# Cached keys of a decode attention step: 32x32 block loads turned by VectorE in place of TensorE transposes

## The reference, cut to what matters

```python
h = rmsnorm(x, g_mix_pre)
proj = h @ w_in                       # q, k, v, xr, gb, gates
k_past = cache_k[l][page_table].reshape(Bs, past_len, N_HEADS, HEAD_DIM)
v_past = cache_v[l][page_table].reshape(Bs, past_len, N_HEADS, HEAD_DIM)
k_all = concatenate([k_past, k]); v_all = concatenate([v_past, v])
logits = einsum('bhqd,bhqjkd->bhqjk', q, kg) * (HEAD_DIM ** -0.5) + bias   # T5 relative bias, masked
p = softmax(logits); o_attn = einsum('bhqjk,bhqjkd->bhqd', p, vg)
o_rnn = rglru(conv(xr)) * gelu(gb)
merged = sigmoid(gate_a) * (o_attn @ w_pa) + sigmoid(gate_r) * (o_rnn @ w_pr)
x = x + rmsnorm(merged @ w_out, g_mix_post)
x = x + rmsnorm((silu(g_) * u_) @ w_down, g_ffn_post)      # from f = rmsnorm(x) @ w_gate_up
```

## Time and profile before

| | |
|---|---|
| runs, median (range) | 795.58 us (795.12 to 795.71) |
| the profiled execution, its own time | 790.97 us |
| its span, first to last instruction | 789.2 us |
| busy: TensorE (PE) | 774.7 us, 98% of the span |
| busy: VectorE (DVE), ScalarE (ACT), GpSimd (POOL) | 473.6, 359.6, 64.4 us |
| TensorE's mean granted clock | 0.997 of full speed |
| DMA traffic | 89.21 MB, mean 113 GB/s |

### The profile page before, as it was taken

One profiled execution on the slowest core, in us unless ns is written; L12 is line 12 of the kernel. 1 busy time (PEld: TensorE's weight loads), 2 busy tenths in 40 slices (PEclk: granted clock), 3 DMA queues, 4 the chain that ended last, 5 costly groups with the idle time before them and its releaser, 6 DMA issues.

```text
span 789.2 us, 16457 instructions
## 1 busy us (share of the span) xinstructions
PE 774.7 (98%) x6100; PEld 735.3 (93%) x6100; DVE 473.6 (60%) x741; ACT 359.6 (46%) x624; POOL 64.4 (8%) x149
## 2 busy tenths in 40 slices
PE   8999999999999999999999999999999999999996
PEld 7988988999899899997799999999999999999995
DVE  5665656746637634774567987778777784222223
ACT  6336435634634632334456555545555563223232
POOL 4501102102011010004000000000000010000000
PEclk9999999999999999999999999999999999999998
DMA  7765235345323224615551333322333143222312
GB/s 213 198 183 157 81 108 149 97 114 132 105 80 82 79 86 129 192 54 180 167 167 47 108 107 106 98 86 84 104 106 106 53 155 106 75 82 84 92 54 114
DMA packets 155201, 89.21 MB, mean 113 GB/s; under 512 B 17093, under 2 KB 148633, under 8 KB 155162
## 3 DMA queue, kind: packets, MB, share of 16 engines
q1 hardware_dynamic: 152350, 81.63, 35.6%
q0 software_dynamic: 2576, 6.45, 2.4%
q10 hardware_dynamic: 236, 0.61, 0.3%
HBM read 81.85 MB, written 6.81 MB: 112 GB/s over the span
## 4 chain that ended last, share of the span: by engine, by line
PE 94%; SPq 3%; issue 1%; DVE 1%; ACT 1%; DMA 0%; DVEq 0%; ACTq 0%
PE ps L865 33%; PE ps L1210 27%; PE ps L1275 17%; PE ps L1109 6%; PE ps L1179 3%; PE ps L964 1%; PE ps L978 1%; PE ps L995 1%; PE ps L937 1%; SPq L563 1%; SPq L569 1%; SPq L553 1%; PE ps L1043 1%; PE ps L1117 1%; PE ps L1008 1%
## 5 line engine op out<-in xcount | busy, mean ns | idle before, releaser
L1821 DVE TENSOR_TENSOR w_lo<-w_raw,w_hi 128x1024 fp32r<-128x1024 f32 (+1 forms) x68 | 80.9, 1192 | 131.0 <-ACT w_hi L1352 130.7
L865 PE MATMUL ps<-xin_hi,w_hi 128*128 128x272 f32 x576 | 126.1, 298 | 0.9 <-DVE xin_lo L1844 0.9
L1352 ACT ACTIVATE w_hi<-w_raw 128x1024 fp32r<-128x1024 f32 (+1 forms) x68 | 69.9, 1030 | 118.6 <-PE ps L1275 82.6
L865 PE MATMUL ps<-xin_hi,w_lo 128*128 128x272 f32 x576 | 120.4, 288 | 0.0
L865 PE MATMUL ps<-xin_lo,w_hi 128*128 128x272 f32 x576 | 120.2, 288 | 0.0
L865 PEld LDWEIGHTS ps<-xin_hi,w_hi 128*128 128x128 f32 x576 | 90.1, 189 | 9.2 <-issue 7.6
L865 PEld LDWEIGHTS ps<-xin_lo,w_hi 128*128 128x128 f32 x576 | 91.0, 188 | 0.0
L865 PEld LDWEIGHTS ps<-xin_hi,w_lo 128*128 128x128 f32 x576 | 90.6, 189 | 0.0
L1275 PE MATMUL ps<-hid_hi,w_hi 128*128 128x272 f32 x352 | 76.0, 291 | 0.4 <-DVE hid_lo L2215 0.4
L1275 PE MATMUL ps<-hid_lo,w_hi 128*128 128x272 f32 x352 | 74.9, 287 | 0.0
L1275 PE MATMUL ps<-hid_hi,w_lo 128*128 128x272 f32 x352 | 74.9, 288 | 0.0
(11 more groups left out here) (338 smaller groups left out, 1756.8 us busy)
## 6 DMA issues: line engine op xcount, KB each, us to landing
w_raw<-in_w_in_dram SPq DMA_DIRECT2D x72, 256.0 KB, 3.2
g_raw<-in_w_gate_up_dram SPq DMA_DIRECT2D x40, 256.0 KB, 3.9
w_raw<-in_w_down_dram SPq DMA_DIRECT2D x40, 256.0 KB, 2.9
u_raw<-in_w_gate_up_dram SPq DMA_DIRECT2D x20, 256.0 KB, 3.1
e_raw<-in_w_gate_up_dram SPq DMA_DIRECT2D x20, 256.0 KB, 4.3
kc<-in_cache_k_dram SPq DMA_DIRECT2D x64, 64.0 KB, 2.1
vc<-in_cache_v_dram SPq DMA_DIRECT2D x64, 64.0 KB, 2.0
wo_raw<-in_w_out_dram SPq DMA_DIRECT2D x12, 256.0 KB, 3.8
```

The costliest lines, as they stand in the source:

```text
L865: mm = e.matmul(ps[:, bank + h, 0:HT], wt[:, kw, :], xt[:, kx, h * HT:h * HT + HT], start=first and wt is wh and xt is xh, stop=last and ( ...
L1352: e.activation((to or w_hi[s])[:, 0:k, :], w_raw[s][:, 0:k, :], ACT.Copy).then_inc(hi_done, count)
L1821: e.tensor_tensor(wl[:, 0:k, :], w_raw[s][:, 0:k, :], wh[:, 0:k, :].bitcast(F32), ALU.subtract).then_inc(lo_done, count)
```

## The change

The keys of pairs 1 to 3 are no longer turned by TensorE. `load_keys` loads a page so that the partition is 32 x (feature block) + (token // 4) and the row holds 4 tokens x 32 features: the source pattern is 4 blocks x 128 tokens x 32 features, in runs of 128 bytes. `keys_turn(f)` on VectorE then turns 32x32 blocks, four pages in one instruction of 128x512, straight from `kc` to `kcT`. In `kcT` token 4i+a of a page then stands at column 32a+i. The bias is copied into that order (4 GpSimd copies for one), the value pages are loaded in that order (4 x 32 rows of 512 bytes), and pair 0, whose keys are still loaded by rows and turned by TensorE, writes the order when it leaves PSUM. A semaphore `kc_turned` takes over from the counts of T_BANK. The key pages of the next pair are issued a few behind each weight tile: in pair 0 four each behind tiles 4 to 7, in pairs 1 and 2 behind tiles 2 to 7 (2, 3, 3, 3, 3, 2), and the wait ahead of them is for this pair's four turns. In pair 0 the groups and `scores_s` stand a little earlier between the matmuls.

```diff
@@ constants @@
-TP_IT = 5 + len(PT_USES)
+TP_IT = 1 + len(PT_USES)
+BLK = 32
+KC_PAGES = (), (), range(0, 2), range(2, 5), range(5, 8), range(8, 11), range(11, 14), range(14, 16)
+KC_PAGES_0 = (), (), (), (), range(0, 4), range(4, 8), range(8, 12), range(12, 16)
@@ helpers @@
+        def cache_cols(f):
+            return kcT[:, 2 * f:2 * f + 2, :].rearrange("p b (n a i) -> p (b n) i a", n=NPG, i=BLK)
+        def cache_turned():
+            return ps[:, T_BANK, :].rearrange("p (n i a) -> p n i a", n=4, i=BLK)
@@ SyncE @@
-            def load_pages(cache, dst, done, it, part):
+            def page_of(cache, it, j):
+                return cache[0].rearrange("n t h d -> n t (h d)")[bass.ds(page[j], 1), :, bass.ds(it * P, P)]
+            def load_keys(it, pages):
+                for j in pages:
+                    e.dma_start(kc[:, j, :], page_of(cache_k, it, j).rearrange("o t (b c) -> b (o t) c", c=BLK)
+                                ).then_inc(kc_in, 16)
+            def load_keys_0():
+                for j in range(DEC_B * NPG):
+                    e.dma_start(kc[:, j, :], page_of(cache_k, 0, j).rearrange("o t c -> t (o c)")).then_inc(kc_in, 16)
+            def load_values(it, part):
                 for j in range(8 * part, 8 * part + 8):
-                    src = cache[0].rearrange("n t h d -> n t (h d)")[bass.ds(page[j], 1), :, bass.ds(it * P, P)]
-                    e.dma_start(dst[:, j, :], src.rearrange("o t c -> t (o c)")).then_inc(done, 16)
+                    e.dma_start(vc[:, j, :], page_of(cache_v, it, j).rearrange("o (i a) c -> a (o i) c", i=BLK)
+                                ).then_inc(vc_in, 16)
...
-                    if j in (5, 6) and not last:
-                        e.wait_ge(s_ready, it * 5 + 1)
-                        load_pages(cache_k, kc, kc_in, it + 1, j - 5)
+                    pages = (KC_PAGES_0 if first else KC_PAGES)[j]
+                    if pages and not last:
+                        e.wait_ge(kc_turned, it * 4 + 4)
+                        load_keys(it + 1, pages)
@@ GpSimd @@
-            e.tensor_copy(bias_s[:, :, 0:PAST], bias_rev[:, :, DEC_T:DEC_T + PAST][:, :, ::-1]).then_inc(consts, 1)
+            for f in range(PAIRS):
+                src = bias_rev[:, f, DEC_T:DEC_T + PAST][:, ::-1].rearrange("p (n i a) -> p n a i", n=NPG, i=BLK)
+                e.tensor_copy(bias_s[:, f, 0:PAST].rearrange("p (n a i) -> p n a i", n=NPG, i=BLK), src).then_inc(consts, 1)
@@ TensorE @@
                 def cache_T(f):
                     if f == 0:
-                        e.wait_ge(kc_in, it * 256 + 256)
-                    tp_wait(f)
+                        e.wait_ge(kc_in, 256)
+                    else:
+                        e.wait_ge(kc_turned, f)
...
-                    cache_T(1); begin(2); part(2, 0, 2); cache_T(2); part(2, 2, 4); cache_T(3); part(2, 4, 8); scores_s()
+                    cache_T(1); begin(2); part(2, 0, 1); cache_T(2); part(2, 1, 3); cache_T(3); part(2, 3, 6)
+                    scores_s(); part(2, 6, 8)
                 else:
-                    begin(0); part(0, 0, 4); cache_T(0); part(0, 4, 8)
-                    begin(1); cache_T(1); part(1, 0, 4); cache_T(2); part(1, 4, 8)
-                    begin(2); cache_T(3); part(2, 0, 5); scores_s(); part(2, 5, 8)
+                    begin(0); part(0, 0, 8)
+                    begin(1); part(1, 0, 8)
+                    begin(2); part(2, 0, 5); scores_s(); part(2, 5, 8)
@@ VectorE @@
+                def keys_turn(f):
+                    if f == 0:
+                        e.wait_ge(kc_in, it * 256 + 256)
+                        e.wait_ge(pv_done, it)
+                    e.transpose(kcT[:, 2 * f:2 * f + 2, :].rearrange("p b k -> p (b k)"),
+                                kc[:, 4 * f:4 * f + 4, :].rearrange("p n c -> p (n c)")).then_inc(kc_turned, 1)
...
                 else:
-                    next_lo(0); cache_copy(1)
-                    next_lo(1); cache_copy(3)
+                    next_lo(0)
+                    keys_turn(0); keys_turn(1)
+                    next_lo(1)
+                    keys_turn(2); keys_turn(3)
                     next_lo(2)
                     k_copy()
```

More of the change, by code:

```diff
@@ L92 @@
 C_ZERO = 8
-C_BIAS = C_ZERO + 1 + DEC_B + 2 * PAIRS
+C_BIAS = C_ZERO + PAIRS + DEC_B + 2 * PAIRS
+BLK = 32
+KC_PAGES = (), (), range(0, 2), range(2, 5), range(5, 8), range(8, 11), range(11, 14), range(14, 16)
+KC_PAGES_0 = (), (), (), (), range(0, 4), range(4, 8), range(8, 12), range(12, 16)
 SERIES = 9
@@ L355, in program @@
         kc_in = sem("kc_in")
+        kc_turned = sem("kc_turned")
         vc_in = sem("vc_in")
@@ L594, in iteration @@
                     if j in (2, 4) and first:
-                        load_pages(cache_v, vc, vc_in, 0, (j - 2) // 2)
-                    if j in (5, 6) and not last:
-                        e.wait_ge(s_ready, it * 5 + 1)
-                        load_pages(cache_k, kc, kc_in, it + 1, j - 5)
+                        load_values(0, (j - 2) // 2)
+                    pages = (KC_PAGES_0 if first else KC_PAGES)[j]
+                    if pages and not last:
+                        e.wait_ge(kc_turned, it * 4 + 4)
+                        load_keys(it + 1, pages)
                 e.wait_ge(mi_free, it * 6 + 3)
@@ L613, in iteration @@
                     e.wait_ge(mi_ready, it * 6 + 3)
-                    load_pages(cache_v, vc, vc_in, it + 1, 0)
-                    load_pages(cache_v, vc, vc_in, it + 1, 1)
+                    load_values(it + 1, 0)
+                    load_values(it + 1, 1)
             load(2, 0, wi[:, :, 2 * 512:2 * 512 + P])
-            for part in range(2):
-                load_pages(cache_k, kc, kc_in, 0, part)
+            load_keys_0()
             load(3, 1, wi[:, :, 3 * 512:3 * 512 + P])
@@ L758, in _ @@
                 own = bias_s[:, f, PAST:KS].rearrange("p (j g t) -> p j g t", j=NJ, g=NG)
-                e.wait_ge(consts, C_ZERO + 1 + DEC_B + 2 * f)
+                e.wait_ge(consts, C_ZERO + PAIRS + DEC_B + 2 * f)
                 e.affine_select(out=own, in_=own, compare_op=ALU.is_ge, fill=NEG,
                                 base=0, pattern=[[-8, NJ], [-GR, NG], [0, DEC_T]], channel_multiplier=1).then_inc(consts, 1)
-                e.wait_ge(consts, C_ZERO + 2 + DEC_B + 2 * f)
+                e.wait_ge(consts, C_ZERO + PAIRS + 1 + DEC_B + 2 * f)
                 e.affine_select(out=own, in_=own, compare_op=ALU.is_ge, fill=NEG,
@@ L933, in cache_T @@
                     if f == 0:
-                        e.wait_ge(kc_in, it * 256 + 256)
-                    tp_wait(f)
+                        e.wait_ge(kc_in, 256)
+                    else:
+                        e.wait_ge(kc_turned, f)
                     for n in range(4):
                         mm = e.transpose(ps[:, T_BANK, n * P:n * P + P], kc[:, 4 * f + n, :], ident[:, :])
-                    mm.then_inc(tp_ready, 1)
+                    mm.then_inc(small_T, 1)
                 def scores_s():
@@ L944, in scores_s @@
                     e.wait_ge(mi_free, it * 6 + 1)
-                    tp_wait(4)
+                    e.wait_ge(kc_turned, it * 4 + 4)
                     e.wait_ge(logits_done, it * 9 + 1)
@@ L973, in probs_T @@
                     e.wait_ge(scaled, it * 8 + (unit(qt, 1 if both else hs) + 1))
-                    tp_wait(5 + n)
+                    tp_wait(1 + n)
                     for i, h in enumerate(range(2) if both else (hs,)):
@@ L983, in probs_T_s @@
                     e.wait_ge(probs_done, it + 1)
-                    tp_wait(4)
+                    tp_wait(0)
                     for n in range(NPG):
@@ L1402, in cache_copy @@
                 def cache_copy(f):
-                    e.wait_ge(tp_ready, it * TP_IT + (f + 1))
-                    e.activation(kcT[:, 2 * f:2 * f + 2, :], ps[:, T_BANK, :].rearrange("p (b k) -> p b k", b=2),
-                                 ACT.Copy).then_inc(tp_free, 1)
+                    e.wait_ge(small_T, f + 4)
+                    e.activation(cache_cols(f), cache_turned(), ACT.Copy).then_inc(kc_turned, 1)
                 def exp_s():
@@ L1418, in probs_copy @@
                     qt, hs = PT_USES[n]
-                    e.wait_ge(tp_ready, it * TP_IT + (5 + n + 1))
+                    e.wait_ge(tp_ready, it * TP_IT + (n + 2))
                     if hs == 2:
@@ L1441, in heads @@
                     e.activation(sp[2][:, :], sp[1][:, :], ACT.Exp, scale=-1.0).then_inc(sp_act, 1)
-                cache_copy(0)
+                    cache_copy(0)
                 next_hi(1)
@@ L1446, in heads @@
                 e.activation(halves(qT[:, :]), two(0), ACT.Copy, scale=DH ** -0.5).then_inc(tile_free[0], 1)
-                cache_copy(2)
+                if first:
+                    cache_copy(2)
                 next_hi(2)
@@ L1453, in heads @@
                 e.activation(halves(vT[:, :]), two(0), ACT.Copy).then_inc(tile_free[0], 1)
```

(13 more changed lines are left out.)

1 line of the change is left out of this document (removed).

## The result

The changed kernel takes 814.2 us (median of 4, 812.5 to 814.6) against 795.35 for the kernel before: 1.0244 times as long, interval 1.021 to 1.0279. The forecast was 813.

What follows compares the result with a forecast made beforehand. TensorE, busy 98% of the span, was taken as the bound. Terms -6.0 + 13.5 + 8.4 + 2 gave +18 us: 809 on the profiled execution, 813 on the median of 795.6; range 792 to 842.

Steps and rivals of the forecast that it cites:

- Transposes removed: On TensorE, twelve groups of transposes go at 0.45 us each: 5.4 us gained.
- pair 0's new order: In pair 0, the 0.86 us wait is covered, `cache_T(2)` waits some 0.3 us: net 0.6 us gained.
- VectorE and GpSimd: Four turns of 0.71 us a pair and four bias copies cost nothing; GpSimd's bounds 0 and 1 us.
- Four engines: On the page loads, 4 of 16 DMA engines carry each page; chance 0.58 at about 12 to 18 ns, 800 to 842.
- Pair 0: Full DMA queue makes TensorE wait at `probs_T(2)` and at pair 1's tiles 0 and 1: 13.5 us.
- Tile 1's 2.0: At pair 1's tile 1, ready at 105.1 where TensorE wants it at 103.1: 2.0 us more wait.
- The price of a small row: A load of a 128-byte row takes one DMA engine 12 ns, with bounds 12 and 25 ns.
- Pairs 1 and 2: Late tile 3 load makes `scores_s` wait 3.7 us, the next tile 0 costs 0.5: 8.4 us for both pairs.
- Clock: After a TensorE wait of 9 us some matmuls run at 1.2 GHz: 2 us, bounds 0 and 5.
- The first rival: Sixteen engines carry a page, nothing queues, `scores_s` waits 2.2 us a pair: -1.6 us, 794 (791 to 797); chance 0.32.

Runs made afterwards that it cites:

- experiment 5: Changed kernel with all pages by whole rows on sixteen engines and no key page ahead of tile 3's load: 785.9 us, ratio 0.9936.
- experiment 1: Changed kernel with all key and value pages moved by whole 512-byte rows on sixteen engines: 794.4 us, ratio 1.0029.
- experiment 2: Changed kernel with only the value pages by whole rows on sixteen engines, keys still on four: 799.15 us, ratio 1.0087.
- experiment 3: Changed kernel with only the key pages of pairs 1 to 3 by whole rows on sixteen engines, values still on four: 794.8 us, ratio 1.0035.
- experiment 4: As all pages on sixteen engines, but key pages of pairs 1 to 3 in 128-byte rows, tokens outermost: 794.8 us, ratio 1.0032.
- the last version: Changed kernel, values and bias in cache order, scores written at stride 4, no key page ahead of tile 3's load, next tile 0's load before value pages: 788.8 us.
- experiment 6: Changed kernel with one edit, no key page ahead of tile 3's load: 806.9 us, ratio 1.0181.
- experiment 7: Changed kernel with the next pair's tile 0 load issued ahead of its 16 value pages: 806.1 us, ratio 1.0185.
- experiment 8: Changed kernel with TensorE's waits filled by extra transposes of the identity: 815.9 us, ratio 1.0301.
- the version of 793.0 us: Changed kernel, values and bias in cache order, turned keys read at stride 32, no key page ahead of tile 3's load: 793.0 us, ratio 1.0006.
- the one with quarters: Values and bias in cache order, each key page of pairs 1 to 3 fetched by four transfers, no key page ahead of tile 3's load: 864.0 us, ratio 1.0905.

## Why the prediction was right, and where it was off

By its steps, against the profiled executions:

- *Transposes removed:* 5.4, and 0.6 from pair 0's new order. The values of a pair (the matmuls that follow the scores) start at 77.51, 141.21, 204.92, 268.63 us in the kernel before and at 77.60, 139.53, 201.47, 263.42 in experiment 5: 1.77 us a pair and nothing in pair 0. So 5.3 and 0: the 0.6 did not come. The 0.86 us wait went, but two waits of 0.27 us at `cache_T` took its place, one for a copy, as expected, and one for the cached keys.
- *VectorE and GpSimd:* nothing expected and nothing found. A turn took 0.68 us (0.71 expected). A wait of 0.47 us for the spread queries of GpSimd shows at the first `scores_s` in experiments 1 and 2, inside the bound of 1 us, and none in the changed kernel.
- *Four engines:* shown, by the packets and by experiments 1 to 4. Sixteen engines with small rows (experiment 4) behave nearly like whole rows: 2.7 and 2.9 us at `scores_s` where these have 2.5.
- *Pair 0:* tile 5 expected to land at 56.1, its split began at 57.14; `probs_T(2)` 2.3 expected, 1.78 measured; tile 0 of pair 1 landed 94.7 expected, 95.67 measured; its wait 9.2 against 9.48. Tile 1's 2.0 measured 0.24, as the half clock at tile 0 covered it; with the clock kept up it was 2.07. The price of a small row, 12 ns, was too high (9.4), that of a whole one on four engines near (25 against 27); the two errors are of opposite sign.
- *Pairs 1 and 2:* 3.7 at each `scores_s`, measured 3.51 and 3.55; 0.5 expected at the next tile 0, measured nothing there and 1.0 and 0.4 at the next tile 1. Of the 3.5, about 2.5 are SyncE's wait for the turned keys, which stays on sixteen engines (2.2 expected there), and 1 is the two slow pages.
- *Clock: the term that was mis-sized.* I took 2 us, after the one wait of 9 us, with bounds 0 and 5. By the rows it fell after three waits, two of them of 3.5 us; TensorE's work in 98 to 104, 120 to 128 and 190 to 196 us (busy time of each two-microsecond stretch by what its clock lacked of 1) lost 2.4 + 3.3 + 1.7 = 7.4 us, 5.3 of it net. I had priced the waits at `scores_s` as their length alone, though nothing in the rows said that 3.5 us is too short for the clock to fall: in the earlier trace rows it is down in 785 to 786 us, and TensorE's last work stands in 782 to 783.

The sum on the profiled execution's own time was 809 (+18), and it took 814.2 (+23.2): 5 short. Measured, its terms are -5.3 for the transposes, 11.5 for waits in pair 0 and at the start of pair 1, 8.4 in the other pairs, and 7.4 for the clock, together 22.0; 1.2 is placed nowhere. So the clock was 5.4 too low and the transposes' gain 0.7 too high; tile 1's wait, which the slow clock covered, was 2 too high. Against the medians the forecast of 813 was near, because the median before (795.6) already held some 4 us that the profiled execution lacks. So the sign, the mechanism and the places are right but for the falls of the clock after `scores_s`, and the last microsecond of agreement is luck. The range, 792 to 842, was wide enough for both signs; the case rests on the steps, not on it.

The first rival (sixteen engines, 794, or -1.6) was put right as a case: experiment 1's profiled execution differs from the kernel before by -0.2, with 2.5 us of wait where 2.2 stood, and its median by +0.29%, which goes with lower mean clocks in its slower executions.

## What to carry to other kernels

Before a DMA's pattern is turned around, count its outermost entries on both sides: with 4 against 128, four engines carried it, and every load behind it on the same queue paid, not the transfer itself. Splitting it into more transfers is no cure where issues are the queue's price (0.78 us each here); leaving the data in memory order and undoing the order in a matmul's output columns was free here, at a stride of four. And price a wait on TensorE with what follows it: here 3.5 us of idling cost up to 3.3 more at half clock.

## What the runs showed of the hardware that I had not expected

- **Two groups of times for one kernel.** Of the 25 executions of the kernel before beside experiments 1 to 4, 19 took 790.8 to 792.1 us, five 794.8 to 796.1 and one 793.1; the mean granted clock is 0.995 to 0.998 in the 19 and 0.989 to 0.991 in the five. Those of the last version lie at 785 (0.996 to 0.997) and 789 (0.991). In the profiled executions of experiments 3, 6, 7 and 8 the granted clock is 0.50 from 12 to 20 us and the first `scores_s` starts at 44.2 to 44.4 us, where the others have 40.0 to 41.3 (and a clock of 1.00, the changed kernel 0.79). No profile of a 795 us execution of the kernel before was taken, so that the two groups of before are the same thing is likely, not shown.
- **The length of a short wait does not decide whether the clock falls.** Half clock came with or just after waits of 2.73 and 2.90 us in experiment 4, 2.39 and 1.96 in experiment 2, and 1.91 in the version of 793.0 us; none came after 2.51 in experiment 1, 2.62 and 2.63 in experiment 6, or 2.90 in experiment 7. What does decide it no run shows. Times spread with it: with two waits of 2.5 us (experiment 1) 790.8 to 797.7 us in four clusters, without them (experiment 5) 785.6 to 786.2 and 789.2 to 789.5.
- **A slow transfer shows first as issue time.** With sixteen engines a key page took 0.47 us to issue (1.88 for four), on four engines up to 1.6; the issuing queue stalls before any waiter does.
- **Reading the keys at a stride had a price, writing the scores at one had none:** the sixteen matmuls took 2.09 us at full clock when they read at 32 columns, and 1.07, as in the kernel before, when they wrote at 4.
- **Closing packets also count unequal transfers:** the 170206, 151582, 170782 and 173086 packets of experiments 2, 3, 4 and the one with quarters, and the 169438 of the changed kernel, follow exactly from the 152350 before with 4 or 16 closing packets a transfer. By that, the Trainium skill's rule that the largest number up to 16 that divides both sides is taken ("DMA: Bandwidth & Descriptors", section "Why a DMA increments its semaphore by 16 and not by 1") holds here for sides of 4 and 128 too.
